# A seven-product gate and up projection begun one tile pair earlier in two of four feed-forward layers, on new halves of the hidden dimension

## The reference

```
h = rms_norm(x, norm_g)                  # 512 x 1024
gate, up = split(h @ w_gu, 2)            # w_gu: 1024 x 5632, each half 512 x 2816
x = x + 0.5 * (silu(gate) * up) @ w_down # w_down: 2816 x 1024
```

## Time and profile before

| | |
|---|---|
| median of three runs | 2163.68 us |
| profiled execution, its own time | 2163.63 us |
| profiled execution, span from first to last instruction | 2161.8 us |
| TensorE busy | 2144.5 us, 99% |
| TensorE weight loads (beside the matmuls) | 1835.3 us, 85% |
| VectorE busy | 1680.9 us, 78% |
| ScalarE busy | 1176.7 us, 54% |
| GpSimd busy | 253.0 us, 12% |
| mean granted TensorE clock | 1.000 |

### The profile page before, as it was taken

One profiled execution on the slowest core, in us unless ns is written; L12 is line 12 of the kernel. 1 busy time (PEld: TensorE's weight loads), 2 busy tenths in 40 slices (PEclk: granted clock), 3 DMA queues, 4 the chain that ended last, 5 costly groups with the idle time before them and its releaser, 6 DMA issues.

```text
span 2161.8 us, 33546 instructions
## 1 busy us (share of the span) xinstructions
PE 2144.5 (99%) x13412; PEld 1835.3 (85%) x13412; DVE 1680.9 (78%) x2546; ACT 1176.7 (54%) x1922; POOL 253.0 (12%) x187
## 2 busy tenths in 40 slices
PE   9999999999999999999999999999999999999999
PEld 6989897777779898989899997777789898977777
DVE  8789697988678796888787787777688886966873
ACT  6536264667556263546355356777555362638672
POOL 3000004000040000040010112000130000030000
PEclk9999999999999999999999999999999999999999
DMA  7454535131135555354554542222135545332211
GB/s 214 123 136 99 151 94 161 40 98 60 46 89 141 124 137 151 84 162 125 176 129 127 122 126 92 77 75 95 50 79 150 137 100 150 98 131 74 79 59 39
DMA packets 249451, 237.75 MB, mean 110 GB/s; under 512 B 4984, under 2 KB 245240, under 8 KB 249296
## 3 DMA queue, kind: packets, MB, share of 16 engines
q1 hardware_dynamic: 208336, 210.25, 30.3%
q0 software_dynamic: 40752, 25.11, 8.7%
q10 hardware_dynamic: 208, 0.24, 0.0%
HBM read 213.79 MB, written 6.32 MB: 102 GB/s over the span
## 4 chain that ended last, share of the span: by engine, by line
PE 91%; DVE 4%; ACT 2%; issue 1%; DMA 0%; SPq 0%; ACTq 0%; DVEq 0%
PE ps L1982 90%; PE ps L1986 1%; DVE sb_wlo L1334 1%; DMA sb_raw<-ffn_w_gu 0%; ACT sb_whi L771 0%; DVE sb_gla_ek L1689 0%; DVE sb_gla_eq L1692 0%; ACT sb_hyb_th L771 0%; ACT sb_lnb L771 0%; DVE sb_gla_cf L1681 0%; DVE sb_gla_xb L1684 0%; DVE sb_gla_d L1669 0%; SPq L737 0%; DVE sb_rb L1965 0%; ACT sb_xh L771 0%
## 5 line engine op out<-in xcount | busy, mean ns | idle before, releaser
L1982 PE MATMUL ps<-sb_xh,sb_whi 128*128 128x512 f32 (+1 forms) x1812 | 625.4, 345 | 3.6 <-issue 1.8
L1982 PE MATMUL ps<-sb_xl,sb_whi 128*128 128x512 f32 (+1 forms) x1812 | 608.8, 337 | 0.1
L1982 PE MATMUL ps<-sb_xh,sb_wlo 128*128 128x512 f32 (+1 forms) x1812 | 606.7, 337 | 0.0
L771 ACT ACTIVATE sb_whi<-sb_raw 128x1024 fp32r<-128x1024 f32 (+1 forms) x368 | 379.9, 1037 | 376.6 <-PE ps L1982 359.8
L1982 PEld LDWEIGHTS ps<-sb_xh,sb_whi 128*128 128x128 f32 x1812 | 344.0, 190 | 56.8 <-issue 20.4
L1982 PEld LDWEIGHTS ps<-sb_xl,sb_whi 128*128 128x128 f32 x1812 | 344.2, 190 | 39.3 <-DVE sb_xl L1354 3.3
L1982 PEld LDWEIGHTS ps<-sb_xh,sb_wlo 128*128 128x128 f32 x1812 | 343.9, 190 | 37.1
L1982 PE MATMUL ps<-sb_ffn_tl,sb_whi 128*128 128x256 f32 x1200 | 339.6, 283 | 0.0
L1982 PE MATMUL ps<-sb_ffn_th,sb_whi 128*128 128x256 f32 x1200 | 339.6, 283 | 0.0
L1982 PE MATMUL ps<-sb_ffn_th,sb_wlo 128*128 128x256 f32 x1200 | 339.6, 283 | 0.0
L1334 DVE TENSOR_TENSOR sb_wlo<-sb_raw,sb_whi 128x1024 fp32r<-128x1024 f32 (+1 forms) x218 | 275.6, 1271 | 49.1 <-ACT sb_whi L771 48.6
(11 more groups left out here) (293 smaller groups left out, 2919.9 us busy)
## 6 DMA issues: line engine op xcount, KB each, us to landing
sb_raw<-ffn_w_gu SPq DMA_DIRECT2D x86, 1024.0 KB, 5.8
sb_raw<-ffn_w_down SPq DMA_DIRECT2D x32, 1024.0 KB, 5.1
sb_raw<-sb_raw POOLq DMA_DIRECT2D x75, 256.0 KB, 4.2
sb_raw<-w_ada SPq DMA_DIRECT2D x12, 1024.0 KB, 7.6
sb_raw<-ffn_w_down SPq DMA_DIRECT2D x16, 768.0 KB, 5.6
sb_raw<-gla_w_in SPq DMA_DIRECT2D x12, 1024.0 KB, 5.5
sb_raw<-diff_w_in SPq DMA_DIRECT2D x12, 1024.0 KB, 5.1
sb_raw<-w_in SPq DMA_DIRECT2D x10, 1024.0 KB, 5.1
```

What stands on the lines that cost most here:

```text
L771: return e.activation(out, in_, func, bias=bias, scale=scale)
L1982: return e.matmul(out, lhsT, rhs, start=start, stop=stop, skip_group_check=skip)
```

## The change

1. `FAST` of the second and fourth FFN begins at pair 2 instead of 3, so the third pair of these two is made with seven products.
2. The halves of the feature dimension are now the even and the odd tiles, in all four FFNs. Step `t` takes the tiles `2t` and `2t + 1`.
3. `SUMS_AT` of the second and fourth FFN is steps 1 and 2 in pair 0 and step 3 in pair 1. Step 0 is done in the output projection ahead: ScalarE scales tiles 0 and 1 at `m` = 5 (`SUMS_AHEAD - 1`), VectorE makes the three sum instructions at `m` = 6. Its high and low parts come with step 1.
4. The scaled tiles of a step lie in the memory of the two gate tiles, no longer beside the first sums.
5. `RING_SKIP` is one less in the second and fourth FFN, so that the banks stand as before from the third down tile of part 0 on.
6. `lambda_products`, three small VectorE instructions, run at the start of pair 3 of the third FFN instead of the end of pair 2.

```diff
-FAST = (tuple(range(4, 22)),) + (tuple(range(3, 22)),) * 3
-SUMS_AT = (((), (0, 1), (2, 3), ()),) + (((0, 1), (2, 3), ()),) * 3
+FAST = (tuple(range(4, 22)), tuple(range(2, 22)), tuple(range(3, 22)), tuple(range(2, 22)))
+SUMS_AT = ((), (0, 1), (2, 3), ()), ((1, 2), (3,)), ((0, 1), (2, 3), ()), ((1, 2), (3,))
+SUMS_AHEAD = 6
-RING_SKIP = (2, 2, 2, 3)
+RING_SKIP = (2, 1, 2, 2)
...
-                x_sum[f] = sb(f"ffn{f}_xs", [128, 8, 256], F32, early)
+                sb(f"before_ffn{f}_xs", [128, 4, 256], F32, early)
+                first_out = sb(f"ffn{f}_xs", [128, 4, 256], F32, early)
...
-            x_out[f] = x_sum[f][:, 4:8, :], ov[:, :, :]
+            x_out[f] = first_out[:, :, :], ov[:, :, :]
...
+            gates = sb(f"ffn{f}_g", [128, 2, S], F32, mem)
+            x_sum[f] = gates[:, :, :].rearrange("p k (c d) -> p (k c) d", d=256)
...
                         for t in SUMS_AT[f][j]:
-                            scaled_x(f, t)
-                            if t:
-                                high_sums(t - 1)
-                            if t == 3:
-                                high_sums(t)
+                            high_step(f, t)
...
+            def high_step(f, t):
+
+                y, th = ffn_mem[f][2], ffn_mem[f][6]
                 if t:
                     w.wait_ge(sem["t_vec"], x_sums_done(f, t - 1))
                 for k in range(2):
+                    act(y[k], x[:, 2 * t + k, :], ACT.Copy,
+                        scale=col("norm_g", NORM_OF_FFN[f] * KT + 2 * t + k)).then_inc(sem["t_act"], 1)
+                for n in {0: (), 3: (2, 3)}.get(t, (t - 1,)):
+                    w.wait_ge(sem["t_vec"], x_sums_done(f, n))
+                    act(th[:, n, :, :], x_out[f][n % 2], ACT.Copy).then_inc(sem["t_act"], 1)
...
+                    if norm is not None and m == SUMS_AHEAD - 1:
+                        w.wait_ge(sem["out_x"], n * KT + 2)
+                        high_step(2 * n + 1, 0)
...
-                a_, b_ = (raw[gate % NRAW][:, k:k + 4, off:off + 128] for k in (0, 4))
-                c_, d_ = (raw[up % NRAW][:, k:k + 4, off:off + 128] for k in (0, 4))
+                a_, b_ = (raw[gate % NRAW][:, k:KT:2, off:off + 128] for k in (0, 1))
+                c_, d_ = (raw[up % NRAW][:, k:KT:2, off:off + 128] for k in (0, 1))
...
+                        if J == 47:
+                            lambda_products()
...
-                            x_sums(f, t)
-                            if t:
-                                low_sums(t - 1)
-                            if t == 3:
-                                low_sums(t)
+                            low_step(f, t)
...
-                        if J == 46:
-                            lambda_products()
...
+            def low_step(f, t):
+
+                th, tl = ffn_mem[f][6:8]
+                x_sums(f, t)
+                for n in {0: (), 3: (2, 3)}.get(t, (t - 1,)):
+                    w.wait_ge(sem["t_act"], high_sums_done(f, n))
+                    e.tensor_tensor(tl[:, n, :, :], x_out[f][n % 2], th[:, n, :, :].bitcast(F32),
+                                    ALU.subtract).then_inc(sem["t_vec"], 1)
...
+                    if norm is not None and m == SUMS_AHEAD:
+                        low_step(2 * n + 1, 0)
...
-                product(run, slots[0], 0, of_x(0, early), 0, True, False).then_inc(sem["t_prod"], 1)
-                product(two, slots[0], 4, of_x(4, early), 4, True, True).then_inc(sem["w_used"], 1)
+                product(run, slots[0], even, of_x(0, early), 0, True, False).then_inc(sem["t_prod"], 1)
+                product(two, slots[0], odd, of_x(1, early), 1, True, True).then_inc(sem["w_used"], 1)
...
-                    e.dma_start(raw[up % NRAW][:, 0:4, off:off + 128], raw[gate % NRAW][:, 0:4, off:off + 128],
+                    e.dma_start(raw[up % NRAW][:, 0:KT:2, off:off + 128], raw[gate % NRAW][:, 0:KT:2, off:off + 128],
                                 accum_op=ALU.add).then_inc(sem[f"s_pre{i % 2}"], 16)
```

More of the change, by code:

```diff
@@ L452, in ffn_memory @@
             th, tl = (sb(f"ffn{f}_{n}", [128, 4, 4, 256], F32R, mem) for n in ("th", "tl"))
-            return ah, al, [g[:, :] for g in gate], up, (one_v, four_five), sums, th, tl
+            return ah, al, tiles_of(gates), up, (one_v, four_five), sums, th, tl
         ffn_mem = []
@@ L2110, in fast_pair, with product @@
                 early, late = slice(0, 256), slice(256, 512)
-                def product(out, slot, t0, parts, ready, start, stop):
-                    for t in range(4):
-                        if ready is not None:
-                            w.wait_ge(sem["x_lo"], 8 * NORM_OF_FFN[f] + ready + t + 1)
+                def product(out, slot, tiles, parts, odd, start, stop):
+                    for t, k in enumerate(tiles):
+                        if odd is not None:
+                            w.wait_ge(sem["x_lo"], 8 * NORM_OF_FFN[f] + 2 * t + odd + 1)
                         else:
@@ L2118, in product, with of_x @@
                         hi, lo = parts(t)
-                        mm(out, whi[slot][:, t0 + t, :], hi, start and t == 0, False, True)
-                        mm(out, whi[slot][:, t0 + t, :], lo, False, False, True)
-                        ins = mm(out, wlo[slot][:, t0 + t, :], hi, False, stop and t == 3, True)
-                    return ins
-                def of_x(k0, half):
-                    return lambda t: (xh[:, k0 + t, half], xl[:, k0 + t, half])
+                        mm(out, whi[slot][:, k, :], hi, start and t == 0, False, True)
+                        mm(out, whi[slot][:, k, :], lo, False, False, True)
+                        ins = mm(out, wlo[slot][:, k, :], hi, False, stop and t == 3, True)
+                    return ins
+                def of_x(odd, half):
+                    return lambda t: (xh[:, 2 * t + odd, half], xl[:, 2 * t + odd, half])
                 def of_sums(k):
@@ L2130, in fast_pair @@
                 slots = [(u + k) % NSLOT for k in range(4)]
+                even, odd, first_four, last_four = range(0, 8, 2), range(1, 8, 2), range(4), range(4, 8)
                 lo_done(w, u)
-                product(run, slots[0], 0, of_x(0, early), 0, True, False).then_inc(sem["t_prod"], 1)
-                product(two, slots[0], 4, of_x(4, early), 4, True, True).then_inc(sem["w_used"], 1)
+                product(run, slots[0], even, of_x(0, early), 0, True, False).then_inc(sem["t_prod"], 1)
+                product(two, slots[0], odd, of_x(1, early), 1, True, True).then_inc(sem["w_used"], 1)
                 lo_done(w, u + 1)
-                product(five_three, slots[1], 0, of_sums(0), None, True, False).then_inc(sem["t_prod"], 1)
+                product(five_three, slots[1], first_four, of_sums(0), None, True, False).then_inc(sem["t_prod"], 1)
                 w.wait_ge(sem["t_cap"], 4 * i + 1)
-                product(run, slots[1], 4, of_sums(2), None, False, False).then_inc(sem["w_used"], 1)
+                product(run, slots[1], last_four, of_sums(2), None, False, False).then_inc(sem["w_used"], 1)
                 lo_done(w, u + 2)
                 w.wait_ge(sem["t_cap"], 4 * i + 2)
-                product(five_three, slots[2], 0, of_x(4, late), 4, False, True).then_inc(sem["w_used"], 1)
+                product(five_three, slots[2], first_four, of_x(1, late), 1, False, True).then_inc(sem["w_used"], 1)
                 lo_done(w, u + 3)
-                product(four, slots[3], 4, of_sums(3), None, True, True).then_inc(sem["t_prod"], 1)
+                product(four, slots[3], odd, of_sums(3), None, True, True).then_inc(sem["t_prod"], 1)
                 w.wait_ge(sem["t_cap"], 4 * i + 3)
-                product(run, slots[3], 0, of_sums(1), None, False, True).then_inc(sem["w_used"], 1)
+                product(run, slots[3], even, of_sums(1), None, False, True).then_inc(sem["w_used"], 1)
                 emptied[banks[0]], emptied[banks[1]] = ("f_join", 2 * i + 2), ("f_join", 2 * i + 1)
```

14 lines of the change are left out of this document (1 added, 13 removed).

## The result

The changed kernel takes 2168.91 us, the median of 11 runs (2168.66 to 2169.64), against 2163.73 for the kernel before (11 runs): 5.18 us more, a ratio of 1.0023 with a 95% interval of 1.0015 to 1.0031. The forecast was 2167.4 with 2162.8 to 2169.8. The time lies in that range, 1.5 above the forecast. The prediction gave 0.65 to a difference within 4.33 us and 0.32 to a slower kernel, above 2168.01; the medians say slower, by 0.9, but the interval is 3.2 to 6.7 us and takes in the 4.33, so it doesn't decide between the two. Some executions of most kernels here, the one before among them, take 1 to 2 us longer than the rest; all are in the medians and intervals. The profiled execution took 2169.07 (span 2167.3), 5.44 more than the one before. All its times are 0.18 later from the first microseconds on; that is taken off where the two are compared.

The account below looks back on a forecast made before the run. TensorE, busy 99%, was taken as the bound. Waits less gains made the second FFN 1.29 and the fourth 2.44 longer, +3.73 on 2163.63 us; with 0.05 to the median, 2167.4, range 2162.8 to 2169.8.

Parts of the forecast that it names:

- What bounds the kernel: In second and fourth FFN TensorE never waits: each matmul less is won in full, each new wait lost in full.
- The gain of 0.80 per pair: Pair 2 of second and fourth FFN: 10.88 us becomes 10.08, a gain of 0.80 each, 1.60 in all.
- Step 0 costs nothing: Output projection ahead: VectorE's three sums at `m` = 6 take 2.7 us, ending 607.9, before the addition at 608.23.
- The third rival: Step 0 blocked by GpSimd: three sums each wait 2.15 us; up to 5 us per FFN, 2177; chance 0.02.
- The three waits of the second FFN: TensorE in pair 2 waits 0.76 for pair 0's `plain_gate`, then 0.65 and 0.68 for ScalarE's copies; FFN 1.29 longer.
- The fourth FFN: Same chain as the second, first wait 0.94 longer, accumulating DMA 0.21 later: 2.44 us longer in all.
- The late accumulating DMA: Fourth FFN: lands after 5.8 us, about 1596.14, where VectorE wants it at 1595.93; 0.21 us more.
- The two copy waits: Pair 2: TensorE waits 0.65 and 0.68 us for ScalarE's copies, carried over from the second to the fourth FFN.
- What costs nothing: Even and odd tiles, DMA order, panel releases, `lambda_products`, first and third FFN: no cost; failed covers under 2 us each.
- Waits hidden: Rival: TensorE's waits in pair 2 are hidden and the gain stays, 2162.1; half-hidden 2162 to 2165; together chance 0.18.
- DMA late: Rival: accumulating DMAs hold VectorE at the weight sums, +0.94 in second FFN, 1.6 in fourth; 2169.9; chance 0.17.
- the signs: If right: breaks near 636 and 1604 ended by `plain_gate`, then two shorter by ScalarE's copies; pair 2 12 to 13 us.

Follow-up runs that it names:

- e3: The whole change in the second FFN only, the fourth FFN's third pair left plain, against the kernel before: 2165.81 us, 2.07 above it.
- e4: The whole change in the fourth FFN only, the second left as before, against the kernel before: 2166.95 us, 3.21 above it.
- e12: Second FFN alone converted, step 0 a unit earlier, both gates, pair 1's product and `fa` low moved ahead; against the kernel before: 2163.07 us, ratio 0.9996.
- e7: Changed kernel with step 0 one output unit earlier (`SUMS_AHEAD` 5 instead of 6): 2168.38 us, 0.53 less than the changed kernel.
- e5: Changed kernel with a free third PSUM bank for pair 2 of the second and fourth FFN, instead of bank 4: 2169.58 us, ratio 1.0026 to the kernel before.
- e1: Only the even and odd halves and the moved scaled tiles, third pairs plain, no step ahead, against the kernel before: 2163.80 us, ratio 1.0001.
- e2: Even and odd halves, moved scaled tiles and step 0 ahead, third pairs plain, against the kernel before: 2164.00 us, ratio 1.0000.
- e6: Changed kernel with all three remaining steps in pair 0 and its `plain_gate` ahead of pair 2's weight sums: 2165.07 us, 3.84 less than the changed kernel.

## Why the prediction was right or wrong

- **What bounds the kernel: right.** Every stall of TensorE in the two places came out at the end, unshortened (5.43 of 5.44 in the trace; `e3` and `e4` add up to the whole).
- **The gain of 0.80 per pair: right.** `e12` shows it almost alone: 0.64 less in the trace, with no stall above 0.15 left in pair 2.
- **Step 0 costs nothing: wrong**, and the largest error in the second FFN. The prediction took the three instructions at 2.7, from a place where it saw one of them held up by GpSimd. They took 605.32 to 609.71, 4.4. That moved the addition of `x` by 1.22, the first scaled copy of step 1 by 0.53, and `plain_gate` to 637.05, where the prediction's 636.11 is 636.29 with the offset: 0.76 late. `e7` takes it back: 0.73 of the first stall, and what is left between starts, 0.75, is the 0.76 that the prediction worked out. The third rival named the mechanism, but at its worst, three whole sums of 2.15. The Trainium skill ("SBUF — State Buffer", section "SBUF: two separate sides") has the shared port pair held for a whole instruction by whichever starts first, and the other blocked. The trace agrees, in that each of the three ended 0.55 or 0.29 after the GpSimd instruction that was running when it started. So a hold follows what is left of that instruction: with 1.23, 0.86 and 1.11 left, the three took 1.09, 0.73 and 0.98 more than alone. The row of 1.40 did not speak against it, and the prediction read it wrongly: both the first and the second instruction there were held, the first by 0.11 only, because its GpSimd instruction was nearly over. Two rows of the kernel before would have given the price:

```profile
607.61 1.29 POOL L2583 TENSOR_TENSOR sb_sqs<-sb_sqs,sb_sq 128x512 f32<-128x512 f32 x1
...
621.52 1.62 POOL L2583 TENSOR_TENSOR sb_sqs<-sb_sqs,sb_sq 128x512 f32<-128x512 f32 x1
```

The instruction at 622.03 in the earlier trace rows ends at 623.43, 0.29 after the second of these. So the last of step 0's three would end 0.29 after the first of them, at about 609.2, an estimate: 1.0 past 608.23, where 1.22 came.

- **The three waits of the second FFN: right in place, cause and order.** Between starts they are 1.48, 0.52 and 0.62, where 0.76, 0.65 and 0.68 stood. The first holds the delay of step 0, and because TensorE came later, the other two are shorter. Left out was the slow second matmul behind each stall, together 0.28. 1.29 + 0.72 - 0.13 - 0.06 + 0.28 = 2.10, against 2.07 measured.
- **The fourth FFN: the first wait nearly right, what follows hidden by something else.** 0.76 + 0.94 + 0.21 = 1.91 was foreseen and 2.20 came. The late accumulating DMA was right in kind and size: VectorE stood 0.24 at the weight sums, and the chain of waits names it. The two copy waits (1.33) were not seen: at the lower clock TensorE itself was late, and pair 2 took 1.57 longer. In `e5`, where the clock stayed at 1.00, TensorE did stop at both copies, 2.65 and 0.48 by the bracket. And pair 1 ends 0.21 later than the second FFN's loss accounts for: in pair 0 a matmul at 1584.19, whose weight load waited for a low part of `x`, starts some 0.16 behind its place. The same 0.16 stands in `e7`, so it isn't the place of step 0 alone that makes it. 2.20 + 1.57 + 0.21 - 0.80 = 3.18, where 2.44 stood.

The DMA in the chain of waits (start, duration), and the weight sum that it ended on VectorE:

```profile
1593.01 5.79 DMA sb_raw<-sb_raw
```

```profile
1598.92 0.69 DVE L1348 TENSOR_TENSOR sb_ffn_sums<-sb_raw 128x512 f32<-128x512 f32 x1 [0.24 <-DMA sb_raw<-sb_raw]
```

- **What costs nothing: right as far as it shows.** `e1` and `e2` are within 0.3 of the kernel before.
- **The rivals.** Waits hidden: fell in this order of the work; `e12` shows that they can be hidden in the second FFN by another one. DMA late: 0.24, as in the forecast. Step 0 blocked: its mechanism acted, at 1.22 of the 5 that it was given for the addition of `x`. Of the signs, the breaks behind `plain_gate` came in both FFNs, those at the copies in the second only.

In short, 1.29 for the second FFN was 2.07, mostly for step 0; 2.44 for the fourth was 3.18, in which the lower clock stood in the place of the copy waits. Both errors went the same way, so none of the nearness is two errors that cancel.

## What to carry to other kernels

Where an engine with no slack stands at the end of a chain of two others, work that is moved away from the chain gains nothing if other work comes into its place: place the new work behind the instruction that releases the full engine, and try another buffer only once the chain is known to be early (`e5` against `e6`). A VectorE instruction with two inputs in SBUF that is moved beside GpSimd work is to be priced from the GpSimd rows at its new place: in these traces it ends 0.55 (128x512) or 0.29 (128x256) after the GpSimd instruction under way at its start. A row from another place, where the two met at another moment, gives the wrong price. And a stage with 0.9 us less slack, like the fourth FFN against the second, may not bear an order that is free in its twin: convert the one that bears it.

## What the hardware showed that was not expected

TensorE's granted clock fell from 1.00 to 0.50 for some 3.4 us within 1.3 us of the end of an idle time of 2.05, in the changed kernel; in `e4` and `e7` it did so after 1.96 and 2.06 at the same place. It stayed at 1.00 after 1.32 in the second FFN, and also, in `e5`, after 2.65:

```profile
1608.00:1610.00 2.00, 2.00 (x19) 2.00 (x17) 0.77 (x2) 1.16 (x3) 0.00 (x0) 1.00 0.00 0
1610.00:1612.90 2.90, 0.25 (x3) 0.05 (x2) 2.28 (x4) 2.83 (x5) 0.00 (x0) 1.00 0.00 0
1612.90:1614.90 2.00, 1.68 (x12) 1.47 (x12) 1.95 (x3) 1.84 (x4) 0.00 (x0) 1.00 0.00 0
1614.90:1617.00 2.10, 1.95 (x16) 1.98 (x17) 2.08 (x3) 1.59 (x4) 0.23 (x1) 1.00 0.04 8
```

So the length of the idle time alone does not decide it; what does stays open. Its price here was small, because at full clock the copies stop TensorE anyway: from the last matmul of pair 1 to the first of pair 3 the changed kernel took 1619.49 - 1605.41 = 14.08, and `e5`, at full clock, 1619.44 - 1605.54 = 13.90.
